# Low parts of weights on GpSimd, written by four instructions of 512 columns in place of one of 2048

## The reference

```python
def first_block(x, ...):
    for layer in range(2):
        xn = rms_norm(x, norm_mix[layer])
        x = x + (even_mixer(xn, ...) if layer == 0 else odd_mixer(xn, ...))
        x = x + jnp.square(relu(rms_norm(x, norm_mlp[layer]) @ w1[layer])) @ w2[layer]
    return rms_norm(x, norm_final)

def second_block(x, mem, ...):
    proj = rms_norm(x, mix_norm_gain) @ w_in
    xa, ga, qm, km, vm, qx, g_logits = split(proj)
    y_a = rg_lru(causal_dwconv(xa, ...), ...) * gelu(ga)
    y_b = moba_attention(qm, km, vm)
    y_c = memory_cross_attention(qx, mem_k, mem_v)
    x = x + (sigmoid(g_logits) * einsum(stack(y_a, y_b, y_c), w_branch)).sum(branches) @ w_out
    h = rms_norm(x, ffn_norm_gain)
    x = x + (gelu(causal_dwconv(h @ w_gate)) * (h @ w_up)) @ w_down
    return rms_norm(x, final_norm_gain)
```

## Time and profile before

| what | value |
|---|---|
| median of 3 runs | 1334.36 us (1332.22 to 1334.56) |
| profiled execution, its own time | 1332.44 us |
| its span (first to last instruction) | 1330.6 us |
| PE busy | 1265.6 us (95%), 10309 matmuls |
| DVE, ACT, POOL busy | 834.4, 621.2, 263.9 us |
| granted TensorE clock, mean | 0.98 |

### The profile page before, as it was taken

How to read it: one execution, slowest core, us unless ns; L and a number is a source line. 1 busy time by engine, 2 the same in 40 slices (tenths; PEclk the granted TensorE clock), 3 DMA queues, 4 the chain that set the end, 5 groups by cost and what they waited for, 6 DMA issues and landing times.

```text
span 1330.6 us, 23858 instructions
## 1 busy us (share of the span) xinstructions
PE 1265.6 (95%) x10309; PEld 1219.8 (92%) x10309; DVE 834.4 (63%) x1108; ACT 621.2 (47%) x761; POOL 263.9 (20%) x103
## 2 busy tenths in 40 slices
PE   7989999999999999998789999989999898999997
PEld 7967889999999999997689999989989888999997
DVE  6667556655565666666756655584777676555653
ACT  5554455544345445444355543435366445444431
POOL 2300130000012111110230000376211364433000
PEclk9999989999999999999989999999999998999998
DMA  9532345555566554544246555643543344555550
GB/s 253 171 127 88 104 137 182 190 188 179 176 224 200 183 179 156 189 156 131 65 127 190 189 176 177 196 159 127 174 149 127 127 159 135 183 190 188 176 176 32
DMA packets 194710, 213.99 MB, mean 161 GB/s; under 512 B 5235, under 2 KB 182718, under 8 KB 194606
## 3 DMA queue, kind: packets, MB, share of 16 engines
q1 hardware_dynamic: 189518, 204.93, 47.7%
q10 hardware_dynamic: 4896, 7.08, 1.8%
q0 software_dynamic: 192, 0.46, 0.1%
HBM read 205.11 MB, written 1.05 MB: 155 GB/s over the span
## 4 chain that ended last, share of the span: by engine, by line
PE 74%; DVE 9%; ACT 7%; issue 5%; POOL 1%; DMA 1%; ACTq 0%; DVEq 0%; POOLq 0%
PE ps L498 67%; ACT whi L918 3%; PE ps L600 2%; PE ps L635 2%; PE ps L608 1%; DVE XL L1334 1%; DVE BIG L1755 1%; ACT SN L980 1%; POOL wlo L1952 1%; DVE XT L1424 1%; DVE XT L1417 1%; DVE BIG L1835 1%; DVE SN L1368 1%; DVE BIG L1751 1%; ACT XH L950 1%
## 5 line engine op out<-in xcount | busy, mean ns | idle before, releaser
L498 PE MATMUL ps<-XH,whi 128*128 128x256 f32 x1704 | 489.0, 288 | 9.3 <-ACT XH L950 9.3
L1300 DVE TENSOR_TENSOR wlo<-raw,whi 128x2048 fp32r<-128x2048 f32 (+1 forms) x151 | 352.6, 2336 | 231.2 <-ACT whi L918 231.0
L498 PE MATMUL ps<-XL,whi 128*128 128x256 f32 x1704 | 485.1, 286 | 2.3 <-DVE XL L1334 1.6
L498 PE MATMUL ps<-XH,wlo 128*128 128x256 f32 x1704 | 483.3, 285 | 0.0
L918 ACT ACTIVATE whi<-raw 128x2048 fp32r<-128x2048 f32 (+1 forms) x189 | 359.5, 1903 | 182.9 <-PE ps L498 156.3
L498 PEld LDWEIGHTS ps<-XH,whi 128*128 128x128 f32 x1704 | 329.7, 194 | 15.4 <-ACT XH L950 11.5
L498 PEld LDWEIGHTS ps<-XL,whi 128*128 128x128 f32 x1704 | 329.2, 194 | 4.3 <-DVE XL L1334 2.9
L498 PEld LDWEIGHTS ps<-XH,wlo 128*128 128x128 f32 x1704 | 329.8, 194 | 0.2
L1952 POOL TENSOR_TENSOR wlo<-raw,whi 128x2048 fp32r<-128x2048 f32 x38 | 176.3, 4645 | 484.6 <-ACT whi L918 484.6
L498 PE MATMUL ps<-HH,whi 128*128 128x256 f32 x832 | 229.5, 283 | 0.0
L498 PE MATMUL ps<-HL,whi 128*128 128x256 f32 x832 | 229.3, 283 | 0.0
(11 more groups left out here) (224 smaller groups left out, 1512.3 us busy)
## 6 DMA issues: line engine op xcount, KB each, us to landing
raw<-in_mlp_w_dram SPq DMA_DIRECT2D x64, 1024.0 KB, 5.3
raw<-in_od_w_in_dram SPq DMA_DIRECT2D x36, 1024.0 KB, 5.3
raw<-in_w_in_dram SPq DMA_DIRECT2D x24, 1024.0 KB, 5.2
raw<-in_w_ffn_gate_dram SPq DMA_DIRECT2D x12, 1024.0 KB, 5.1
raw<-in_w_ffn_up_dram SPq DMA_DIRECT2D x12, 1024.0 KB, 5.1
raw<-in_w_ffn_down_dram SPq DMA_DIRECT2D x12, 1024.0 KB, 5.1
raw<-in_ev_w_in_dram SPq DMA_DIRECT2D x6, 1024.0 KB, 12.1
TB<-TA ACTq DMA_DIRECT2D x96, 64.0 KB, 4.2
```

What stands on the lines that cost most here:

```text
L498: m = pe.matmul(to, l[c][a], r[c][b], start=first and k == 0, stop=last and k == 3 * n - 1)
L1300: dve.tensor_tensor(wlo_of(n), raw_of(n), f32(whi_of(n)), ALU.subtract).then_inc(*tell(s_wlo, ("wlo", n)))
```

## The change

POOL's `low` issues, in place of one subtraction over 2048 columns, four over 512 columns each, one after the other, on the flat buffers. The two waits stand ahead of the first one, and the event ("wlo", n) on the last one, so PE is told once per slab as before. Nothing else in the program differs: the 38 instructions of L1952 become 152, in the same places of POOL's order; no other engine's instructions, no buffers and no waits move.

```diff
                 once.wait_ge(*at(("raw", n)))
                 once.wait_ge(*at(("whi", n)))
-                pool.tensor_tensor(wlo_of(n), raw_of(n), f32(whi_of(n)), ALU.subtract).then_inc(*tell(s_pool_wlo, ("wlo", n)))
+                lo, r, hi = (t[:, 0:2048] for t in (wlo[n % RAW], raw[n % RAW], whi[split_at(n) % PARTS]))
+                for q in range(4):
+                    v = slice(512 * q, 512 * q + 512)
+                    m = pool.tensor_tensor(lo[:, v], r[:, v], f32(hi[:, v]), ALU.subtract)
+                m.then_inc(*tell(s_pool_wlo, ("wlo", n)))
```

## The result

The changed kernel takes 1314.8 us (median of 4 runs, 1313.79 to 1315.45), beside 1334.46 us for the kernel before (4 runs): a ratio of 0.9853, with a 95% interval of 0.9836 to 0.987, or 17 to 22 us less. The prediction was 1317 us, with a range of 1308 to 1328. The profiled execution took 1313.79 us, its span is 1312.0 us, 18.6 us shorter than the one before; the mean granted clock is 0.984.

What follows compares the result with a forecast made beforehand. PE holds most of the chain; DVE's SBUF-only instructions wait out POOL's whole slabs and delay PE. Terms sum to 16.0 us off the profiled 1332.44: 1316.4, or 1318.4 by the median; forecast 1317 us, range 1308 to 1328.

Steps and rivals of the forecast that it cites:

- terms 1 and 2: Inputs of the first and second MLP: shorter DVE waits gain 1.2 us at the first, 1.8 and 0.9 at the second.
- term 4: The recurrence and the attention behind it: `alibi` is loaded 4.4 us sooner, and all 4.4 us reach the end.
- Term 3: The convolution: sixteen DVE instructions take turns of 1.45 us with POOL's pieces, 1.8 us gained.
- Term 5: The merging: PE's wait for L1401 hangs behind a blend that meets POOL, 1.0 us gained.
- Term 6: The output product: L1839, held up beside POOL, stands ahead of PE's wait for POOL's low part; 2.3 us gained.
- Term 7: Input of the feed-forward part: a DVE pair that loses 4.4 us beside POOL loses less, 2.6 us gained.
- half absorbed: Rival: only direct waits pay, the long chains at the recurrence and feed-forward input give nothing; 1325 us, chance 0.18.
- More than one turn per gap: Rival: DVE gets in more than once between two POOL pieces, since POOL's start is slow; 1308 us, chance 0.08.
- One block: Rival: POOL's four pieces keep DVE out together, every stall 0.4 us longer; 1337 us, chance 0.05.
- Starving: Rival: turns cost POOL so much that low parts come late and the convolution's turns lengthen; 1339 us, chance 0.05.
- of the first kind: DVE instructions that read and write SBUF alone: claimed to wait until POOL's instruction is over, up to 4.6 us.

## Why the prediction was right

Right in the mechanism: DVE gets in between two of POOL's instructions, one each, at 1.42 us a turn (1.45 forecast), and an undisturbed slab takes 5.05 us (5.0). Of the lines that the prediction named, none takes more than 1.62 us in after. The sum, 16.0 us, was 3.6 short of the measured 19.6, and it is made of errors with both signs: 3.9 us too much in terms 1 and 2, some 5 too little in term 4. So that the total came this close is in part luck, and the sum has no term for the clock, which makes up 5.9 of the 19.5 us that the two traces differ by behind 850 us.

- *Terms 1 and 2, the MLP inputs: 3.9 forecast, none measured.* Of the first, "loses most of a microsecond again" was the step that failed: the next pair lost 2.0 us, since the sum of squares stands right behind the last piece. For the second, the waits of DVE got shorter by 1.1 us (1.8 forecast) and 1.7 us (0.9 forecast), but the pieces alone in that stage gave nothing that could be measured; the lower clock there is what the trace of after shows, and not proven to be the cause.
- *Term 3, the convolution: 1.8 forecast, 2.5 measured*, and 2.5 by the two traces. The count of turns at 1.42 us was right.
- *Term 4, the recurrence: 4.4 forecast, 7.9 measured alone, 9.5 in the trace of after.* "I take 4.4 for `alibi`" was right: against PE the load starts 4.4 us sooner in after, with the recurrence's pieces alone and with those of the whole stage. PE's product of slab 133 holds the scan as forecast: in after the instruction ahead of it waits 0.69 us for it. What failed stands behind that. The load landed 1.5 us quicker, for which there was no term; why, no run shows. "From there to 1049 us the chain runs over ACT and DVE alone" was wrong: the blend that met slab 149 was held by POOL, and the 4.0 us of PE's wait hung on it too. And "6.2 us" to give back was too small a ceiling: besides the 2.17 and 4.0 us, PE was idle for another 1.3 us in the attention, and the pause of 4.0 us was followed by a stretch at a lower clock, 1.7 us more. That adds up to 9.2, and to 7.2 without the 2.0 us that a whole slab 149 keeps, which is near the 7.9 of the recurrence's pieces alone.
- *Term 5, 1.0 forecast:* PE's wait for L1401 fell from 1.0 to 0.6, so 0.4. *Term 6, 2.3 forecast:* the wait for POOL's low part is gone, L1839 takes 0.93 and 0.94; the trace gives 3.0 for terms 5 and 6 together. *Term 7, 2.6 forecast:* 3.5 by the trace. The direct part, PE's wait for XH, fell by 2.5, from 4.1 to 1.6; the other 1.0 comes behind that wait, where the clock, for which there was no term, was low before (below); in after it is 1.00 from 1092 to 1100 us. The three terms' slabs alone gave 6.9 beside 5.9.

```profile
1108.00:1112.00 4.00, 2.72 (x9) 0.50 0.00 0
1112.00:1116.00 4.00, 4.00 (x26) 0.72 0.00 0
```

- *The rest of the feed-forward part at nothing:* confirmed by its own run.

Of the rivals, half absorbed is out: its terms 4 and 7 gave more than forecast, not nothing. More than one turn per gap is out where the rows show the turns: DVE gets one, and waits for the next piece. One block is out for the changed kernel, but shown at one place in three of the experiments. Starving doesn't happen with four pieces, for no wait of PE for a low part is left; it begins with eight.

## What to carry to other kernels

Look for instructions of one engine that take far longer than the same line elsewhere, lay the other engine's rows beside them, and cut the long instruction where the two meet; the gain follows the length of the piece until the turns cost the engine that is cut its own lead. Where a chain ends in a pause of PE, count the lower clock behind the pause as well as the pause, and look right ahead of the pause for one more held-up instruction before the whole of it is put down to the chain. A shorter wait on one instruction can move its successor into the next collision, so follow at least two instructions behind each one that gets earlier.

## What the runs showed of the hardware that was not expected

- Between back-to-back instructions of POOL, DVE mostly gets one turn, but not always: at one place it waited for the rest of a piece of 256 columns and nine more (6.76 us in the first L1334 of the pair, in two kernels), and for the rest of one of 512 and three more (5.05 us), with an arrival 0.30 us into a piece where 0.28 us in another kernel got a turn behind that piece. What decides it stays open.
- A turn costs POOL 0.19 us with pieces of 512 columns (1.48 us in place of 1.29), and a cut slab costs 0.4 us (5.05 in place of 4.6).
- A pause of PE of 4.0 us was followed by 4 us at 0.67 of the clock; one of 2.0 us at the same place was not, in the trace of the recurrence's pieces alone.
- Not every DVE instruction within SBUF is held up, as the prediction's "of the first kind" would have it: the reciprocal L1770 takes 3.35 us beside POOL's slab (924.57 us before) and 3.35 us behind POOL's row (934.41 us before).
